# The dense products of a three-layer model kernel on one core: moving rows read, and accumulators written, from the last column to the first

## Chip, core and metric

One core of a Trainium2 chip runs the whole program in one launch. The metric is the device time of that launch in microseconds (us), the median of several executions. A profile is one further execution, recorded by the hardware profiler. In the profile PE is TensorE's matmuls, PEld its weight loads, DVE VectorE, ACT ScalarE, POOL GpSimd and SP the engine that issues most of the DMAs. Line numbers (L167) are lines of the kernel file.

## The reference

The input x is 1 x 1024 tokens x 1024 channels. Two blocks of a first model and one block of a second model follow one another, all in float32:

```python
for i in range(2):                       # first model
    xn  = rms_norm(h, norm_mix[i])
    mix = hawk_block(xn, ...) if i == 0 else rwkv7_time_mix(xn, ...)
    h = h + mix
    h = h + swiglu(rms_norm(h, norm_ffn[i]), ffn_w_in[i], ffn_w_out[i])
    h = h + (p[i] @ ple_w_proj[i]) * sigmoid(rms_norm(h, norm_ple[i]) @ ple_w_gate[i])
h = rms_norm(h, norm_final)
# second model, one block
proj = rms_norm(h, g) @ w_in             # split in u, z, q, k, v, z_attn
h = h + rms_norm(concat(s5(u) * silu(z), window_attention(q, k, v) * silu(z_attn)) @ w_out, g2)
h = h + sigmoid(h @ w_gate + b) * (p_2 @ w_proj)
```

Nearly all arithmetic lies in the `@` products with weights of 1024 to 2816 rows and up to 5632 columns, over 1024 tokens.

## The kernel before

**Layout.** Activations are held transposed: channels on the 128 partitions, the T = 1024 tokens along the free dimension, one row tile of 128 channels after another (`[P, KD, T]`). A dense product takes 128 x 128 pieces of the weight as the stationary operand and a row tile of activations as the moving operand, in two halves of HALF = 512 tokens, each of which goes to one accumulator bank of 128 x 512 float32 in `g.ps`.

**Three passes.** To keep near-float32 accuracy with the one-pass float32r format, each weight is split into a high and a low part (`whi`, `wlo`) and each activation as well (`xh`, `xl`). A product is the sum of whi x xh, whi x xl and wlo x xh. So for each 128 x 128 piece of weight there are six matmuls: three passes times two halves, all into the same pair of banks.

**Four places issue them.** `product` (L167) serves the projections of all blocks; `unit` (L416) the last blocks of a product whose sum of squares is taken on the way, and the output product of the feed-forward network; `combined` (L1047) the input product of the feed-forward network, written as a Strassen-like scheme of seven products on sums and differences of quarters, each in one half (`x[n][:, k, :]` has 512 columns); `piece` (L2423) the first pieces of the RWKV output product, between the steps of the recurrence. All other matmuls (`ident`, `head_mean`, the recurrence, the attention, the state space model) are written out elsewhere with float32 or bfloat16 operands.

**What sets the order.** Each engine has its own instruction list, written by hand, with semaphore waits. SP loads weight blocks in pairs (`load_blocks`, L106), POOL splits them (`split_blocks`, L117 to L120) once the block before the last is done, ACT and DVE make the high and low rows of the activations and read the finished accumulators. Two pairs of banks take turns (`banks(g, 2 * s)`, s = 0 or 1), so one is read while the other fills.

**Two other products matter for what follows.** In the state space model, `steps(ap)` views a row of 1024 tokens as four interleaved sequences, every fourth token:

```python
def steps(ap):
    return ap.rearrange("p (c j) -> p j c", j=STEP)      # STEP = 4, 256 tokens each
```

`s5_drive_pe` (L3561) streams such a row of 256 tokens as the moving operand, with 32 partitions as contraction, four in different row groups of the array. `within` (L3599) streams one or two of them (256 or 512 columns) over all 128 partitions. Both are float32, both step 4 elements, 16 bytes, from one token to the next, and both write contiguous columns. `across` (L3612) reads 255 contiguous float32 columns and writes 255 contiguous columns of a bank from an odd column on (`i % 2 * NCH + 1`).

Of the kernel before, what the change touches and what calls it, by code (L numbers as in the profile page):

```python
# [13 lines left out]
P = 128  # L14
T = 1024
D = 1024
KD = D // P
HALF = 512
# [137 lines left out]
        nc.tensor.matmul(g.ps[:, b, :], g.ident[:, 0:P // 2].bitcast(BF16), rows, start=True, stop=True)  # L156


def product(nc, g, s, units, xh, xl, acc, at=0, ready=None, start=True, stop=True):

    for kt in range(units):
        if ready is not None:
            ready(kt)
        c = (at + kt) * P
        for n, (w, x) in enumerate(((g.whi, xh), (g.whi, xl), (g.wlo, xh))):
            for hf in (0, 1):
                last = nc.tensor.matmul(acc[:, hf, :], w[:, s, c:c + P], x[:, kt, hf * HALF:(hf + 1) * HALF],  # L167
                                        start=start and kt == 0 and n == 0, stop=stop and kt == units - 1 and n == 2)
    return last


def paired(pe, nc, g, first, units, xh, xl, acc, tail=None, between=None, lead=0):

    pe.wait_ge(g.w_split.sem, first + 2)
    pe.wait_ge(g.acc_free.sem, first)
    keep_busy(nc, g, 7, lead)
    for kt in range(units):
        pe.wait_ge(g.x_split.sem, g.x_split.base + kt + 1)
        for s in (0, 1):
            last = product(nc, g, s, 1, xh[:, kt:kt + 1, :], xl[:, kt:kt + 1, :], acc[s], at=kt, start=kt == 0, stop=kt == units - 1)  # L180
            if kt == units - 1:
                if s == 1 and tail is not None:
                    last = tail()
                last.then_inc(g.block_done.sem, 1)
        if between is not None and kt == KD // 2:
            between()
# [16 lines left out]
def banks(g, b):  # L203

    return g.ps[:, b:b + 2, :]
# [49 lines left out]
def sums_pe(pe, nc, g):  # L255

    pe.wait_ge(g.sq_used.sem, g.sq_used.base + KD)
    for j in range(NT):
        ins = nc.tensor.matmul(g.ps[:, 6, j:j + 1], g.sumsq[:, j * P:(j + 1) * P], g.ones[:, 0:1], start=True, stop=True)  # L259
        if j == NT // 2 - 1:  # L260
            keep_busy(nc, g, 7, 2)
    ins.then_inc(g.ss_done.sem, 1)


def spread_pe(pe, nc, g, tmp):

    pe.wait_ge(g.diag_ready.sem, g.diag_ready.base + 1)
    for hf in (0, 1):
        ins = nc.tensor.matmul(g.ps[:, 6 + hf, :], g.ones[:], flat(tmp.diag[:, 4 * hf:4 * hf + 4, :]), start=True, stop=True)  # L269
    ins.then_inc(g.bc_done.sem, 1)  # L270
# [140 lines left out]
def unit(nc, g, s, at, hi, lo, acc, start, stop):  # L411

    c = at * P
    for n, (w, x) in enumerate(((g.whi, hi), (g.whi, lo), (g.wlo, hi))):
        for hf in (0, 1):
            last = nc.tensor.matmul(acc[:, hf, :], w[:, s, c:c + P], x[:, hf, :], start=start and n == 0, stop=stop and n == 2)  # L416
    return last


# [116 lines left out]
def hawk_in(nc, g, block, m):  # L536
# [33 lines left out]
    def _(pe):  # L570
# [18 lines left out]
        for kt in range(1, KD):  # L589
            if kt == KD // 2:  # L590
                spread_pe(pe, nc, g, tmp)
            ins = unit(nc, g, 1, kt, halves(xh[:, kt, :]), halves(xl[:, kt, :]), banks(g, 2), False, kt == KD - 1)
# [309 lines left out]
def tile_slot(i):  # L902
    return i % FFN_SLOTS


def ffn(nc, g, block, mem, layer):
# [25 lines left out]
    def slot(n):  # L932
        if n in whole:
            h, l, at = whole[n]
            return h[:, at, :], l[:, at, :]
        s, c = shared[n]
        return g.whi[:, s, c:c + HALF], g.wlo[:, s, c:c + HALF]
# [6 lines left out]
    acc = {n: g.ps[:, 4 + n % 4, :] for n in range(PAIR)}  # L944
# [93 lines left out]
    @block.tensor  # L1038
    def _(pe):
        def combined(m, n, acc, ready=None):  # L1040
            hi, lo = slot(n)
            pe.wait_ge(g.weight_low.sem, m * PAIR + (g.weight_low.base - PAIR + n + 1))
            for k in range(KD // 2):
                if ready is not None:
                    pe.wait_ge(g.t_low.sem, g.t_low.base + ready + k + 1)
                for i, (w, x) in enumerate(((hi, mem.hi), (hi, mem.lo), (lo, mem.hi))):
                    last = nc.tensor.matmul(acc, w[:, k * P:(k + 1) * P], x[n][:, k, :], start=k == 0 and i == 0, stop=k == KD // 2 - 1 and i == 2)  # L1047
            last.then_inc(g.product_done.sem, 1)

        def pair(m, ready):  # L1050
            pe.wait_ge(g.fourth_part.sem, m + (g.fourth_part.base - 1))
            combined(m, A11, acc[A11])
            pe.wait_ge(g.up_part.sem, m * 2 + g.up_part.base)
            combined(m, S2_, acc[S2_], ready.get(T2_))
            pe.wait_ge(g.gate_sum.sem, m * 2 + g.gate_sum.base)
            combined(m, A12, acc[A12])
            pe.wait_ge(g.third_part.sem, m + (g.third_part.base - 1))
            combined(m, S3_, acc[S3_], ready.get(T3_))
            pe.wait_ge(g.first_part.sem, m + g.first_part.base)
            combined(m, S1_, acc[S1_], ready.get(T1_))  # L1060
            pe.wait_ge(g.second_part.sem, m + g.second_part.base)
            combined(m, A22, acc[A22], ready.get(T4_))
            pe.wait_ge(g.gate_sum.sem, m * 2 + (g.gate_sum.base + 1))
            combined(m, S4_, acc[S4_])

        def out_block(grp, s, kt_ready=None, kt_used=None, acc=None):
            tiles = tiles_of[grp]
            for n, i in enumerate(tiles):
                if kt_ready:
                    pe.wait_ge(g.tile_low.sem, g.tile_low.base + i + 1)  # L1070
                at = tile_slot(i)
                last = unit(nc, g, s, n, mem.tile_hi[at], mem.tile_lo[at], acc, n == 0, n == len(tiles) - 1)
                if kt_used and n < len(tiles) - 1:
                    last.then_inc(g.tile_used.sem, 1)
            last.then_inc(g.block_done.sem, 1)

        pe.wait_ge(g.w_split.sem, first + 1)
        pe.wait_ge(g.acc_free.sem, first - 1)
        for kt in range(KD):
            if kt == KD - 2:  # L1080
                sums_pe(pe, nc, g)
            pe.wait_ge(g.x_split.sem, g.x_split.base + kt + 1)
            last = unit(nc, g, 0, kt, rows.hi[kt], rows.lo[kt], banks(g, 0), kt == 0, kt == KD - 1)
        last.then_inc(g.block_done.sem, 1)
        pe.wait_ge(g.w_split.sem, first + 2)
        pe.wait_ge(g.acc_free.sem, first)
        for kt in range(KD):
            if kt == 2:
                spread_pe(pe, nc, g, tmp)
            last = unit(nc, g, 1, kt, rows.hi[kt], rows.lo[kt], banks(g, 2), kt == 0, kt == KD - 1)  # L1090
        last.then_inc(g.block_done.sem, 1)
        pe.wait_ge(g.rstd_ready.sem, g.rstd_ready.base + 1)
        pair(1, {T2_: 0, T3_: 4, T1_: 8, T4_: 12})
        with pe.Fori(2, last_pair + 1) as m:
            pair(m, {})
        for grp, fo in enumerate(first_out):
            def wait_block(q, s):
                pe.wait_ge(g.w_split.sem, q * 2 + (fo + s + 1))
                pe.wait_ge(g.acc_free.sem, q * 2 + (fo + s - 1))

            wait_block(0, 0)
            out_block(grp, 0, kt_ready=True, acc=banks(g, 0))
            wait_block(0, 1)
            out_block(grp, 1, acc=banks(g, 2))
            with pe.Fori(1, KD // 2 - 1) as q:
                for s in (0, 1):
                    wait_block(q, s)
                    out_block(grp, s, acc=banks(g, 2 * s))
            wait_block(KD // 2 - 1, 0)
            out_block(grp, 0, acc=banks(g, 0))  # L1110
            wait_block(KD // 2 - 1, 1)
            out_block(grp, 1, kt_used=grp == 0, acc=banks(g, 2))
# [936 lines left out]
def rw_core(nc, g, block, nxt, small, mk, xh, xl):  # L2049
# [19 lines left out]
    sw, a, r, kx, v, c, e1, e2, kk, t1 = (nxt[:, n, :] for n in range(10))  # L2069
    at, bt, kt, rt = (now[:, n, :] for n in range(4))  # L2070
# [140 lines left out]
    def _(pe):  # L2211
# [206 lines left out]
        def piece(s, i):  # L2418
            kt, n, hf = i // 6, i % 6 // 2, i % 2
            if i % 6 == 0:  # L2420
                pe.wait_ge(g.x_split.sem, g.x_split.base + kt + 1)
            w, x = ((g.whi, xh), (g.whi, xl), (g.wlo, xh))[n]
            nc.tensor.matmul(banks(g, 2 * s)[:, hf, :], w[:, s, kt * P:(kt + 1) * P], x[:, kt, hf * HALF:(hf + 1) * HALF],  # L2423
                             start=kt == 0 and n == 0, stop=False)

        pe.wait_ge(g.y1_ready.sem, g.y1_ready.base + KD)
# [8 lines left out]
        for i in range(30, 36):  # L2435
            piece(0, i)
# [1914 lines left out]
```

## Time and profile before

| | |
|---|---|
| median of 3 executions | 3548.92 us (3545.87 to 3551.94) |
| the profiled execution's own time | 3547.82 us |
| its span, first to last instruction | 3546.0 us |
| mean granted TensorE clock over the span | 0.982 of full speed |
| PE busy | 3405.1 us, 96% of the span |
| PEld / DVE / POOL / ACT busy | 78% / 56% / 45% / 34% |

The span and the time differ by 1.8 us, which lies around the program. PE is the busiest engine by far in every stage. A matmul's row in the trace has a start and a duration; matmuls overlap in the pipeline, so the duration of one says how long it takes through the array, and the distance between starts of neighbours says what one costs in a stream.

### The profile page before, as it was taken

Reading aid. Unit: us, or ns where it says so; the run is one execution under the profiler, and the core shown is the slowest. Engines: PE = TensorE matmul, PEld = TensorE weight load, DVE = VectorE, ACT = ScalarE, POOL = GpSimd, SP = SyncE. Lnnn points to the kernel's source line nnn. Section 1 sums busy time; section 2 is a strip of 40 time slices with the busy share of each in tenths; the row PEclk is TensorE's granted clock in tenths of the full one; section 3 lists DMA queues with packets and bytes.
Section 4 is the critical chain, followed back from the end, with each engine's and each line's share of the span. In section 5 each row is a group of like instructions: output and inputs, shape, how many; then the busy total and the mean of one; then the engine's idle time right before and its main releaser. Section 6 shows DMA issues by size and latency. Waiting matters only on the chain. (4 is left out here: it accounts for less than half of the span.)

```text
span 3546.0 us, 61071 instructions
## 1 busy us (share of the span) xinstructions
PE 3405.1 (96%) x25028; PEld 2748.4 (78%) x25028; DVE 1984.6 (56%) x2398; ACT 1194.9 (34%) x1597; POOL 1590.5 (45%) x1148
## 2 busy tenths in 40 slices
PE   7998999999999999999999999999999999999989
PEld 5886778888888777888787877888888887674767
DVE  6886565556224652226767647555542458868452
ACT  4654233333102362226465524333310231242221
POOL 3442377775333323334344425877633323560352
PEclk9998999999999999999999999999999999999999
DMA  2111122224311142241212211222332113111212
GB/s 103 48 49 38 33 87 79 80 89 152 109 42 56 40 179 95 95 147 39 85 46 86 68 37 48 88 89 78 111 128 88 52 42 119 61 48 42 101 43 76
DMA packets 74063, 274.58 MB, mean 77 GB/s; under 512 B 8208, under 2 KB 8592, under 8 KB 73360
## 3 DMA queue, kind: packets, MB, share of 16 engines
q1 hardware_dynamic: 68112, 250.79, 20.8%
q10 hardware_dynamic: 5760, 20.97, 1.5%
q8 instruction: 153, 2.51, 0.3%
q14 instruction: 38, 0.31, 0.0%
HBM read 207.77 MB, written 63.96 MB: 77 GB/s over the span
## 5 line engine op out<-in xcount | busy, mean ns | idle before, releaser
L117 POOL TENSOR_TENSOR gap<-ones 128x1 f32<-128x1 f32 x150 | 46.0, 307 | 1238.8 <-PE ps L167 774.4
L120 POOL TENSOR_TENSOR wlo<-wraw,whi 128x1024 fp32r<-128x1024 f32 (+3 forms) x150 | 391.6, 2611 | 12.5
L893 DVE TENSOR_TENSOR h<-ps,h 128x1024 f32<-128x1024 f32 (+1 forms) x56 | 68.5, 1223 | 288.9 <-PE ps L416 259.6
L167 PE MATMUL ps<-xh,whi 128*128 128x512 f32 x640 | 203.0, 399 | 21.6 <-ACT rw_stage L1888 5.1
L167 PE MATMUL ps<-xl,whi 128*128 128x512 f32 x640 | 199.2, 393 | 0.0
L167 PE MATMUL ps<-xh,wlo 128*128 128x512 f32 x640 | 198.7, 392 | 0.0
L1007 POOL TENSOR_TENSOR wlo<-wraw,whi 128x512 fp32r<-128x512 f32 x126 | 166.3, 1335 | 52.6 <-ACT whi L1130 52.6
L118 POOL TENSOR_SCALAR whi<-wraw 128x1024 fp32r<-128x1024 f32 (+3 forms) x150 | 178.9, 1192 | 0.0
L384 ACT ACTIVATE sq<-h 128x1024 f32<-128x1024 f32 x32 | 34.0, 1061 | 394.1 <-DVE h L893 304.0
L2200 POOL TENSOR_TENSOR rw_levels<-rw_levels,rw_masks 128x512 f32<-128x512 f32 x64 | 87.2, 1378 | 177.2 <-PE ps L2289 140.8
L167 PEld LDWEIGHTS ps<-xh,whi 128*128 128x128 f32 x640 | 119.7, 190 | 56.6 <-issue 8.9
L1007 POOL TENSOR_TENSOR ffn_wl<-ffn_wsum,ffn_wh 128x512 fp32r<-128x512 f32 x84 | 111.6, 1328 | 110.7 <-ACT ffn_wh L1130 110.6
L167 PEld LDWEIGHTS ps<-xl,whi 128*128 128x128 f32 x640 | 121.3, 190 | 25.9
L167 PEld LDWEIGHTS ps<-xh,wlo 128*128 128x128 f32 x640 | 121.2, 189 | 25.8
L1288 DVE TENSOR_TENSOR sum_of_squares<-ffn_part,sq 128x512 f32<-128x512 f32 x84 | 132.6, 1578 | 9.3
L1130 ACT ACTIVATE whi<-wraw 128x512 fp32r<-128x512 f32 x126 | 79.2, 630 | 168.9 <-POOL wraw L1002 90.3
L1047 PE MATMUL ps<-xh_sums,whi 128*128 128x512 f32 x336 | 130.9, 390 | 2.2 <-ACT ffn_part L1143 2.2
L1047 PE MATMUL ps<-xh_sums,wlo 128*128 128x512 f32 x336 | 130.7, 389 | 0.0
L1047 PE MATMUL ps<-xl_sums,whi 128*128 128x512 f32 x336 | 130.7, 389 | 0.0
L433 DVE TENSOR_TENSOR sum_of_squares<-sum_of_squares,sq 128x1024 f32<-128x1024 f32 x48 | 93.7, 1951 | 56.9 <-ACT sq L384 38.7
L416 PE MATMUL ps<-xh_sums,whi 128*128 128x512 f32 x384 | 118.4, 390 | 0.4 <-POOL wlo L120 0.4
L416 PE MATMUL ps<-xh_sums,wlo 128*128 128x512 f32 x384 | 118.3, 389 | 0.0
(673 smaller groups left out, 9535.0 us busy)
## 6 DMA issues: line engine op xcount, KB each, us to landing
wraw<-w_ffn_in SPq DMA_DIRECT2D x88, 512.0 KB, 3.5
ffn_hidden<-sum_of_squares SPq DMA_DIRECT2D x44, 512.0 KB, 2.6
rw_next<-rw_kept SPq DMA_DIRECT2D x40, 512.0 KB, 5.1
wraw<-w_ffn_out SPq DMA_DIRECT2D x32, 512.0 KB, 3.6
ffn_stage<-ffn_hidden SPq DMA_DIRECT2D x30, 512.0 KB, 4.9
rw_kept<-rw_stage SPq DMA_DIRECT2D x24, 512.0 KB, 2.7
rw_kept<-rw_stage ACTq DMA_DIRECT2D x24, 512.0 KB, 2.7
wraw<-w_ple SPq DMA_DIRECT2D x16, 640.0 KB, 3.8
```

Of the source, the lines that this page charges most:

```text
L117: nc.gpsimd.tensor_tensor(g.gap[:, 0:1], g.ones[:, 0:1], g.ones[:, 0:1], ALU.mult)
L118: nc.gpsimd.tensor_scalar(g.whi[:, s, 0:w], g.wraw[:, s, 0:w], 1.0, 0.0, ALU.mult, ALU.add).then_inc(g.w_hi.sem, 1)
L120: nc.gpsimd.tensor_tensor(g.wlo[:, s, 0:w], g.wraw[:, s, 0:w], g.whi[:, s, 0:w].bitcast(F32), ALU.subtract).then_inc(g.w_split.sem, 1)
L167: last = nc.tensor.matmul(acc[:, hf, :], w[:, s, c:c + P], x[:, kt, hf * HALF:(hf + 1) * HALF], start=start and kt == 0 and n == 0, stop=s ...
L416: last = nc.tensor.matmul(acc[:, hf, :], w[:, s, c:c + P], x[:, hf, :], start=start and n == 0, stop=stop and n == 2)
L433: nc.vector.tensor_tensor(g.sumsq[:], g.sumsq[:], sq[:, s, :], ALU.add).then_inc(g.sq_used.sem, 1)
L893: nc.vector.tensor_tensor(ht, flat(banks(g, acc + 2 * s)), ht, ALU.add).then_inc(g.acc_free.sem, 1)
L1007: nc.gpsimd.tensor_tensor(packed(lo), raw[n], packed(hi).bitcast(F32), ALU.subtract).then_inc(g.weight_low.sem, 1)
L1047: last = nc.tensor.matmul(acc, w[:, k * P:(k + 1) * P], x[n][:, k, :], start=k == 0 and i == 0, stop=k == KD // 2 - 1 and i == 2)
L1130: nc.scalar.activation(packed(slot(n)[0]), raw[n], ACT.Copy).then_inc(g.weight_high.sem, 1)
L1288: nc.vector.tensor_tensor(hid[:, hf * HALF:(hf + 1) * HALF], (u3, up1)[hf], gated[hf], ALU.mult).then_inc(g.half_ready.sem, 1)
L2200: nc.gpsimd.tensor_tensor(halved(Nm[:, h]), twice(Nc[:, h]), mask_wide(f"off{b}"), ALU.mult).then_inc(g.off_ready.sem, 1)
```

## The change

A helper `turned` reverses the free dimension of an access pattern. The four places that issue the dense products apply it to the moving operand and to the accumulator. Column 511 of the moving half is read first and its result goes to column 511 of the bank, and so on down to column 0. The stationary operand, the number of instructions, their order, all waits and all readers of the accumulators stay as they are: compared without line numbers, the instruction lists of all engines are the same before and after.

```diff
+def turned(ap):
+
+    return ap[:, ::-1]
+
+
 def product(nc, g, s, units, xh, xl, acc, at=0, ready=None, start=True, stop=True):
...
-                last = nc.tensor.matmul(acc[:, hf, :], w[:, s, c:c + P], x[:, kt, hf * HALF:(hf + 1) * HALF],
+                last = nc.tensor.matmul(turned(acc[:, hf, :]), w[:, s, c:c + P], turned(x[:, kt, hf * HALF:(hf + 1) * HALF]),
...
-            last = nc.tensor.matmul(acc[:, hf, :], w[:, s, c:c + P], x[:, hf, :], start=start and n == 0, stop=stop and n == 2)
+            last = nc.tensor.matmul(turned(acc[:, hf, :]), w[:, s, c:c + P], turned(x[:, hf, :]), start=start and n == 0, stop=stop and n == 2)
...
-                    last = nc.tensor.matmul(acc, w[:, k * P:(k + 1) * P], x[n][:, k, :], start=k == 0 and i == 0, stop=k == KD // 2 - 1 and i == 2)
+                    last = nc.tensor.matmul(turned(acc), w[:, k * P:(k + 1) * P], turned(x[n][:, k, :]), start=k == 0 and i == 0, stop=k == KD // 2 - 1 and i == 2)
...
-            nc.tensor.matmul(banks(g, 2 * s)[:, hf, :], w[:, s, kt * P:(kt + 1) * P], x[:, kt, hf * HALF:(hf + 1) * HALF],
+            nc.tensor.matmul(turned(banks(g, 2 * s)[:, hf, :]), w[:, s, kt * P:(kt + 1) * P], turned(x[:, kt, hf * HALF:(hf + 1) * HALF]),
                              start=kt == 0 and n == 0, stop=False)
```

## Rows read from the trace of the kernel before

**Rows 1.** The page, busy time of each engine: us, share of the span, instructions.
```profile
span 3546.0 us, 61071 instructions
PE 3405.1 (96%) x25028; PEld 2748.4 (78%) x25028; DVE 1984.6 (56%) x2398; ACT 1194.9 (34%) x1597; POOL 1590.5 (45%) x1148
```

**Rows 2.** Windows: length, busy us (instructions) by engine, granted clock, DMA share, GB/s.
```profile
700.00:1300.00 600.00, 586.36 (x2579) 478.18 (x2578) 291.38 (x276) 172.45 (x203) 258.12 (x197) 1.00 0.26 90
1600.00:2060.00 460.00, 426.24 (x11426) 365.45 (x11419) 316.61 (x588) 249.08 (x365) 177.53 (x114) 0.94 0.19 63
2060.00:2900.00 840.00, 830.68 (x3664) 684.00 (x3663) 429.62 (x449) 229.82 (x322) 449.58 (x346) 1.00 0.24 80
```

**Rows 3.** Waits of PE: waiter <- releaser, us in total, times, longest.
```profile
PE ps L167 <- POOL wlo L120: 17.1, 5, 6.6
PE ps L156 <- PEq L3962: 11.9, 1, 11.9
```

**Rows 4.** Windows over the whole span, by line: L167, L1047, L416, then L2423.
```profile
0.00:3546.00 3546.00, 1256.77 (x5328) 1008.41 (x5328) 0.98 0.23 77
...
0.00:3546.00 3546.00, 802.43 (x3528) 661.64 (x3528) 0.98 0.23 77
...
0.00:3546.00 3546.00, 726.76 (x3168) 594.71 (x3168) 0.98 0.23 77
...
0.00:3546.00 3546.00, 21.14 (x72) 12.35 (x72) 0.98 0.23 77
```

**Rows 5.** Timeline of PE in the feed-forward product: start us, duration us, what.
```profile
600.16 0.39 PE L1047 MATMUL ps<-xl_even,ffn_wh 128*128 128x512 f32 x1
600.39 0.39 PE L1047 MATMUL ps<-xh_even,ffn_wl 128*128 128x512 f32 x1
...
611.72 0.39 PE L1047 MATMUL ps<-xl_sums,whi 128*128 128x512 f32 x1
611.95 0.39 PE L1047 MATMUL ps<-xh_sums,wlo 128*128 128x512 f32 x1
```

**Rows 6.** The chain that ended last, in order of time: start, us, what.
```profile
3421.03 21.41 POOL h L3884 x7
...
3456.94 81.91 PE ps L167 x360
...
3541.50 1.23 DVE h L3950
```

**Rows 7.** Timeline of PE, float32 products on contiguous rows.
```profile
2955.94 1.88 PE L3078 MATMUL ps<-sum_of_squares,ones 128*128 128x512 f32 x4
2957.66 1.88 PE L3078 MATMUL ps<-b_high,ones 128*128 128x512 f32 x4
```

**Rows 8.** Timeline of PE, state space model.
```profile
3217.69 9.25 PE L3599 MATMUL ps<-b_low,s_kernel 128*128 128x512 f32 x12
3226.87 3.65 PE L3612 MATMUL ps<-s_state,s_ct 128*32 128x255 f32 x64
...
3197.68 3.82 PE L3561 MATMUL ps<-b_low,h 32*128 32x256 f32 x32
```

**Rows 9.** By line: durations ns min/median/max, first and last start, forms.
```profile
L3599 PE MATMUL ps<-b_low,s_kernel x48: 629/1078/1147, 3217.7 to 3279.5; 128*128 128x512 f32 x32, 128*128 128x256 f32 x16
L3078 PE MATMUL ps<-sum_of_squares,ones x4: 591/592/592, 2955.9 to 2957.2; 128*128 128x512 f32 x4
L3561 PE MATMUL ps<-b_low,h x256: 624/627/692, 3197.2 to 3257.5; 32*128 32x256 f32 x128
L3150 PE MATMUL ps<-h,at_vtok x120: 379/379/430, 3053.9 to 3183.0; 128*64 128x256 f32 x120
L3612 PE MATMUL ps<-s_state,s_ct x256: 378/378/635, 3226.9 to 3286.7; 128*32 128x255 f32 x128
```

## The prediction, made before the changed kernel ran

> **What bounds the kernel now.** I read the busy time of each engine first. PE is busy for 3405.1 of 3546.0 us [rows 1]. The windows say that this is no average over unlike stages: PE is busy for 586.36 of 600 us in the Hawk output and feed-forward part, 830.68 of 840 us in the second layer's feed-forward and what follows, and even in the recurrence of the RWKV block, with 11426 small matmuls, 426.24 of 460 us [rows 2]. The clock is granted in full in the first and the last of these and at 0.94 in the recurrence. All that PE does not use is 3546.0 - 3405.1 = 141 us, in many short pieces: the largest total is 17.1 us for the low weights that POOL makes, the next 11.9 us before the first matmul [rows 3]. So the question is what the dense matmuls cost in a stream, and how many there are.
>
> How many: 5328 + 3528 + 3168 + 72 = 12096 [rows 4]. What one costs: in the feed-forward product the starts run from 600.16 to 611.95 us over 52 matmuls, 11.79 / 52 = 0.2267 us each [rows 5]. The 0.39 us beside each start is the time through the array, and is no cost in a stream. At the end of the program the chain of waits holds 360 of them in one piece of 81.91 us, 0.2275 us each, with only short DVE and ACT work behind [rows 6]. Together 12096 x 0.2267 = 2742 us: 81% of PE's busy time and 77% of the span are dense products, which sit on the path that sets the end nearly everywhere. Whatever one of them gains or loses is multiplied by 12096, and hardly anything hides it: 0.59 ns each is 7.1 us, 0.2% of the time, which is about what a measurement of this kernel can tell from no change.
>
> How near they are to the plain streaming rate: four float32 records of 128 x 512, each of which streams its 512 columns in two passes, start at 2955.94 and the next four at 2957.66 us, so one takes 0.430 us, a pass of 512 contiguous columns 0.215 us [rows 7]. That float32 record really is two passes is read from durations: 592 ns at 512 columns against 379 ns at 256, a difference of 213 ns for 512 column passes [rows 9]. A dense matmul at 0.2267 us is one such pass and 12 ns more. It has no slack in its stream: if the operand is delivered more slowly, the matmul is slower by just that.
>
> **The change, part by part.** No instruction is added, removed or moved, and no wait changes. DMAs, the work of DVE, ACT and POOL, and the stationary loads are as before. Three things change inside each of the 12096 matmuls.
>
> (a) The moving half is read downwards. The trace has no row of a downward read, so I bound it by its neighbours. The upper end is the moving operand that steps by 16 bytes. The state space products at L3599 have 12 records from 3217.69 us on, 8 of 512 and 4 of 256 columns, a width of ten records of 512; the next product starts at 3226.87 us [rows 8, 9]. That is 9.18 / 10 = 0.918 us for one of 512 columns; taken only to the start of the last record (3217.69 + 9.25 - 0.63 = 3226.31, 9.5 widths) it is 0.907. I take 0.91, against 0.430 on contiguous rows. The durations say the same: 1078 against 592 ns [rows 9]. Per pass of 512 columns that is 0.455 against 0.215, or +0.24 us. The product at L3561, also at step 16 bytes, has 32 records in 3.82 us, so (3.82 - 0.63) / 31 = 0.103 us each; four run beside each other in row groups, so four records of 2 x 256 column passes take 0.412 us [rows 8], +0.20 us on 0.215. The lower end is nothing: a backward row uses all four words of every 16 bytes, like a forward row and unlike the stepped one. If what costs is that each element lies in 16 bytes of its own, direction costs nothing; if what gives the full rate is an operand recognised by its step of exactly one word, a step of minus one is like any other and costs +0.20 to +0.24 us.
>
> (b) The accumulator is written downwards, on 12096 instructions, two thirds or more of which add to what is there. Here the trace has one row that speaks. L3612 writes from an odd column on, so that its neighbouring columns fall across pairs of words, and adds to the bank. Its 64 records take 3.65 us, (3.65 - 0.38) / 63 = 0.0519 us each, four beside each other in column groups: 0.208 us for 510 column passes, the full rate [rows 8], and its duration of 378 ns is the 379 ns of the aligned product at L3150 [rows 9]. So the writer doesn't need an even start for its rate. A backward write has the same two words in each pair, in the other order. Between no cost and a write that takes each word alone (half the rate, +0.21 us by the 0.215 us of a pass) I take no cost.
>
> (c) The start of each operand moves to the other end of its row. That could cost or save a fixed time per instruction. The nearest row is the 12 ns by which a dense matmul exceeds a bare pass [rows 5, 7]; I bound it by -12 and +12 ns and take 0, since the odd start of L3612 shows no fixed cost either.
>
> The sum that I forecast: 12096 x (0 + 0 + 0) = 0. The profiled execution's own time, 3547.82 us, stays, and it stands 1.1 us below the median of the three runs, so I predict the median, 3549 us.
>
> **A rule that speaks against it.** The row for writes in which neighbouring words don't follow upwards in a pair is L3612, at the full rate. The Trainium skill, page "PSUM — Partial Sum Buffer", Specifications, says of PSUM's 8-byte lines that "any non-contiguous AP slows matmuls significantly". Read by the letter, a pattern with step -1 is not a contiguous one, and the change would pay on each matmul; that reading is rival 1. The same skill, page "SBUF — State Buffer", in the passage on SBUF cachelines, gives the reason as accesses that stay in one line of 16 bytes, at least two per line, which a backward row does; by it the sum stays at 0. The stepped rows at about half the rate agree with both, and no row separates them.
>
> **Rival 1: the backward stream runs at the stepped rate (slower).** Place: inside every dense matmul, on the read, the write or both. For it: step 16 bytes does cost +0.20 to +0.24 us per 512 columns, and no row shows a negative step at the full rate. Against it: what the stepped rows lack, several elements per 16 bytes, the backward rows have, and the writer takes an odd start for free. Price: 12096 x 0.24 = 2903 us, so 3548 + 2903 = 6451 us; by L3561's 0.20 us it is 2419 us and 5967 us. The other engines would have slack and some of PE's 141 us of waits would close, at most that. It decides as soon as 30 of the 12096 matmuls run at this rate (30 x 0.24 = 7.2 us, 0.2%); since all have the same form, it is all or none: near 0, or 2.4 to 2.9 ms.
>
> **Rival 2: a small fixed price per instruction (slower).** The first fetch or the last write of a backward row could cost a cycle or more. The decision point is 0.59 ns each. A doubling of the 12 ns surplus would be 12096 x 0.012 = 145 us, 3693 us. More likely in this case is a nanosecond or two: 12 to 24 us, 3561 to 3573 us. Against it: the odd start of L3612 shows none.
>
> **Rival 3: the surplus goes (faster).** The 12 ns above a bare pass appear where a weight load runs under each matmul. If the moving stream and the weight load meet less often when one runs backwards, up to 145 us would go: 3404 us. Nothing in the trace points to it: the spacing is the same over all operands, in whatever place of memory they lie.
>
> **Rival 4: it doesn't do what it says.** If the reversal were dropped on both sides when the instruction is encoded, the result is the same and so is the time. It can't be told from the forecast by the time, and is counted with it.
>
> **How the numbers follow.** Forecast and rival 4: 0.73, at 3549 us, within 0.2%. Rival 1: 0.17, at 5970 to 6450 us. Rival 2: 0.07, at 3556 to 3693 us. Rival 3: 0.03, 3404 to 3541 us. So faster 0.03, same 0.73, slower 0.24. The range must leave out no more than 2 in 10: it takes the forecast with the spread of the runs before and rival 2 whole, 3538 to 3695 us, and leaves out rival 1 and most of rival 3. Likeliest alone: 3542 to 3556 us.
>
> **What would show each step.** In the profile after, dense rows of 0.39 us starting 0.227 us apart, PE busy 3405 us and the last 360 products in about 82 us say that (a) to (c) are right. Under rival 1 the durations would read 0.59 to 0.63 us, the starts 0.43 to 0.47 us apart, the loads of DVE, ACT and POOL would be unchanged and their shares nearly halved. Under rival 2 or 3 the spacing would differ from 0.2267 us in the third digit, alike on all four lines. The untouched rows, L3078 at 0.430 and L3599 at 0.91 us, should stay in every case. The prediction is wrong if the reader or the writer knows only an upward step as contiguous.

## The result: 1.8% slower, 6.7 ns on each dense matmul

| | before | after |
|---|---|---|
| median | 3550.43 us (3545.87 to 3556.33, 4 runs) | 3615.28 us (3613.18 to 3619.95, 4 runs) |
| ratio | | 1.0183, 95% interval 1.0165 to 1.0202 |
| span of the profiled execution | 3546.0 us | 3618.1 us |

The change costs 64.9 us between the medians, 72.1 us between the two profiled spans (the profiled execution of the changed kernel was the longest of its four). The page of the changed kernel, to be set beside [rows 1]:

```profile
span 3618.1 us, 61071 instructions
PE 3490.9 (96%) x25028; PEld 2759.5 (76%) x25028; DVE 1984.8 (55%) x2398; ACT 1194.8 (33%) x1597; POOL 1572.7 (43%) x1148
```

The instruction counts are the same on every engine, DVE and ACT are as busy as before, and PE has 85.8 us more. Its idle time shrank from 140.9 to 3618.1 - 3490.9 = 127.2 us, so 13.7 us of idle time closed while the products became slower. 85.8 - 13.7 = 72.1 us, the whole difference.

Where PE's time comes from is told by the windows over the span, by line, to be set beside [rows 4] (the lines are L172, L1052, L421 and L2428 now):

```profile
0.00:3618.10 3618.10, 1289.79 (x5328) 1011.88 (x5328) 0.98 0.22 76
...
0.00:3618.10 3618.10, 825.42 (x3528) 662.72 (x3528) 0.98 0.22 76
...
0.00:3618.10 3618.10, 748.11 (x3168) 596.55 (x3168) 0.98 0.22 76
...
0.00:3618.10 3618.10, 21.39 (x72) 12.38 (x72) 0.98 0.22 76
```

They rose by 33.0, 23.0, 21.4 and 0.2 us, 77.6 us together, that is 6.2, 6.5, 6.7 and 3.5 ns for each matmul. The mean granted clock was 0.982 before and 0.980 in this execution, 0.981 and 0.982 in the other three, so it is not the cause; it may be part of the 8.2 us that all other matmuls were busy longer (85.8 - 77.6). The timeline of the feed-forward product, the place of [rows 5] (first and last of 54 rows; start, duration, what):

```profile
599.62 0.40 PE L1052 MATMUL ps<-xh_sums,wlo 128*128 128x512 f32 x1
...
611.99 0.40 PE L1052 MATMUL ps<-xl_even,ffn_wh 128*128 128x512 f32 x1
```

12.37 us over 53 distances are 0.2334 us each, against 0.2267 before: +6.7 ns. The last 360 products in the chain of waits take 6.6 ns longer each, where [rows 6] have 81.91 us:

```profile
3526.67 84.29 PE ps L172 x360
```

12096 x 6.67 ns = 80.6 us is what the streams of dense products cost more; the rest of the way to 72.1 and 64.9 us is idle time that closed and the spread of the executions. The untouched product of [rows 8] still takes 9.25 us for its 12 records.

### The profile page after: what moved, and what is told of

Its sections match the earlier page's. It is cut to its first block and busy times, and to the rows that moved or that the text cites. A ratio compares the mean times of both kernels' runs of the same rounds, so it can differ in the third digit from the quotient of the medians.

```text
span 3618.1 us, 61071 instructions
## 1 busy us (share of the span) xinstructions
PE 3490.9 (96%) x25028; PEld 2759.5 (76%) x25028; DVE 1984.8 (55%) x2398; ACT 1194.8 (33%) x1597; POOL 1572.7 (43%) x1148
## 5 line engine op out<-in xcount | busy, mean ns | idle before, releaser
L172 PE MATMUL ps<-xh,whi 128*128 128x512 f32 x640 | 207.4, 406 | 20.1 <-ACT rw_stage L1893 4.9
L172 PE MATMUL ps<-xl,whi 128*128 128x512 f32 x640 | 204.2, 402 | 0.0
L172 PE MATMUL ps<-xh,wlo 128*128 128x512 f32 x640 | 204.1, 401 | 0.0
L172 PEld LDWEIGHTS ps<-xh,whi 128*128 128x128 f32 x640 | 120.5, 191 | 57.1 <-issue 8.1
L172 PEld LDWEIGHTS ps<-xl,whi 128*128 128x128 f32 x640 | 122.0, 191 | 29.8
L172 PEld LDWEIGHTS ps<-xh,wlo 128*128 128x128 f32 x640 | 121.9, 190 | 29.5
L1052 PE MATMUL ps<-xh_sums,whi 128*128 128x512 f32 x336 | 133.6, 398 | 0.4 <-ACT ffn_part L1148 0.4
L1052 PE MATMUL ps<-xl_sums,whi 128*128 128x512 f32 x336 | 133.5, 397 | 0.0
L1052 PE MATMUL ps<-xh_sums,wlo 128*128 128x512 f32 x336 | 133.5, 397 | 0.0
L438 DVE TENSOR_TENSOR sum_of_squares<-sum_of_squares,sq 128x1024 f32<-128x1024 f32 x48 | 92.7, 1932 | 56.8 <-ACT sq L389 38.6
L421 PE MATMUL ps<-xl_sums,whi 128*128 128x512 f32 x384 | 121.1, 397 | 0.0
L421 PE MATMUL ps<-xh_sums,wlo 128*128 128x512 f32 x384 | 121.1, 397 | 0.0
```

Source lines behind the costliest of these rows:

```text
L172: last = nc.tensor.matmul(turned(acc[:, hf, :]), w[:, s, c:c + P], turned(x[:, kt, hf * HALF:(hf + 1) * HALF]), start=start and kt == 0 an ...
L421: last = nc.tensor.matmul(turned(acc[:, hf, :]), w[:, s, c:c + P], turned(x[:, hf, :]), start=start and n == 0, stop=stop and n == 2)
L438: nc.vector.tensor_tensor(g.sumsq[:], g.sumsq[:], sq[:, s, :], ALU.add).then_inc(g.sq_used.sem, 1)
L1052: last = nc.tensor.matmul(turned(acc), w[:, k * P:(k + 1) * P], turned(x[n][:, k, :]), start=k == 0 and i == 0, stop=k == KD // 2 - 1 and ...
```

## Experiments

### Read or write?

Two kernels with one half of the change each. Both leave the columns of every dense product mirrored within their half, so their outputs are not the reference's, but they do the full work.

```diff
-    last = nc.tensor.matmul(turned(acc[:, hf, :]), w[:, s, c:c + P], turned(x[:, hf, :]), ...)
+    last = nc.tensor.matmul(acc[:, hf, :], w[:, s, c:c + P], turned(x[:, hf, :]), ...)          # read only
+    last = nc.tensor.matmul(turned(acc[:, hf, :]), w[:, s, c:c + P], x[:, hf, :], ...)          # write only
```

> Only the moving operand is read from the last column to the first; the accumulators are written forward, so within each half of 512 tokens every dense product lands mirrored and the output is not the reference's. The changed kernel's dense matmuls start 0.2334 us apart instead of 0.2267 (+6.7 ns). Theory R (the price is in the backward read): dense starts 0.233 us apart and +60 to +72 us over before, as in the changed kernel. Theory W (it is in the backward write): 0.2267 us apart, within 0.2% of before. Theory S (a share in each): about half, +30 to +36 us.

> Only the accumulators are written from the last column to the first, the moving rows are read forward; the products land mirrored within each half, so the output is not the reference's. Theory R: 0.2267 us apart, within 0.2% of before. Theory W: 0.233 us apart, +60 to +72 us. Theory S: +30 to +36 us. If the price is only paid where read and write directions agree, both this and the read-only kernel stay at before.

Read only: 3610.3 us against 3549.09, ratio 1.0173 (1.0156 to 1.0190). Write only: 3551.69 us, ratio 1.0004 (0.9994 to 1.0013). The price is in the backward read: 61.2 us of the 64.9, and the two ratios' intervals overlap. Writing the accumulator backwards costs nothing that these runs can see, with the operand read forward or backward, so theory R stands and W and S fall.

### Is it a price of each matmul, with nothing to hide it?

```diff
-  last = nc.tensor.matmul(acc, w[:, k * P:(k + 1) * P], x[n][:, k, :], ...)
+  last = nc.tensor.matmul(acc[:, ::-1], w[:, k * P:(k + 1) * P], x[n][:, k, :][:, ::-1], ...)
```

> Read and write backward in the feed-forward input product alone (3528 of the 12096 dense matmuls), the result is the reference's. If the price is one of each matmul and nothing hides it: 3528 x 6.7 ns = 24 us, less what idle time of PE takes up, so +18 to +24 us. If instead it is paid mostly elsewhere (at waits, in other stages): under +10 us.

3571.37 us, ratio 1.0063 (1.0046 to 1.0080), +22.3 us for 3528 of the matmuls. The full change has +64.9 us for 12096, which in proportion would be 18.9 us. So the price goes with the number of matmuls, and little hides it.

### What about the form of the access?

```diff
 def turned(ap):
-    return ap[:, ::-1]
+    return ap.rearrange("p (a b) -> p a b", a=2)[:, ::-1, :]
```

> In the place of backward columns all dense products read and write columns 256 to 511 first and then 0 to 255, both forward (the result is the reference's). If any change of the form of the access or of its first column costs, as much as the backward form or more: +60 us. If it is the negative step of the read: no difference, within 0.2% of before.

3549.84 us, ratio 0.9993 (0.9983 to 1.0002). Two runs of columns in swapped order cost nothing, so the change of the form is not the cause. Of another first column this run says less: column 256 lies 4 x 64 words on, and further below a shift by 64 words turns out to change nothing, while shifts by 1 to 48 words do.

### Streams of one kind of matmul

> The kernel before, unchanged in its result, with streams of 48 (float32: 24) matmuls of one kind each appended at its end, each on a line of its own. Base: forward read and write of 512 columns in float32r, expected 0.2267 us apart; both backward 0.2334. Theory F (a fixed price per instruction, for the start or end of a backward stream): at 256 columns the backward stream is also 6.7 ns dearer. Theory C (a slightly lower rate per column): at 256 columns half of it, 3.3 ns. Theory E (what costs is where a read starts in its line of memory): forward reads that start at the second, third or fourth word show the same price, and the backward ones that start there differ among themselves. Theory L (weight loads meet the backward stream): with one weight tile for all, the difference shrinks. A forward read at step 2 in 256 columns: 0.12 us apart if lines decide, 0.23 if only step one is fast; at step 4 about 0.23 by the rows of L3599. bfloat16 and float32 streams: the same +6.7 ns if the price is the instruction's, nothing if it belongs to float32r.

Each stream is one row of the timeline, and the distance of two rows, divided by 48, is the cost of one matmul. Forward, backward, backward read alone, backward write alone, all 512 columns in float32r (the first holds a slow start, so the forward value of 226.7 ns is taken from the second forward stream of this kernel, with the accumulation started and stopped at each matmul):

```profile
3560.98 11.27 PE L164 MATMUL ps<-xh,whi 128*128 128x512 f32 x48
3572.09 11.37 PE L167 MATMUL ps<-xh,whi 128*128 128x512 f32 x48
3583.30 11.37 PE L170 MATMUL ps<-xh,whi 128*128 128x512 f32 x48
3594.50 11.06 PE L173 MATMUL ps<-xh,whi 128*128 128x512 f32 x48
3605.39 5.92 PE L176 MATMUL ps<-xh,whi 128*128 128x256 f32 x48
3611.15 5.85 PE L179 MATMUL ps<-xh,whi 128*128 128x256 f32 x48
3616.83 5.84 PE L182 MATMUL ps<-xh,whi 128*128 128x256 f32 x48
...
3639.32 11.04 PE L191 MATMUL ps<-xh,whi 128*128 128x512 f32 x48
3650.20 11.37 PE L194 MATMUL ps<-xh,whi 128*128 128x512 f32 x48
```

Backward 11.21 / 48 = 233.5 ns, backward read 233.3, backward write 226.9. L176 and L179 are 256 columns, forward 120.0 and backward 5.68 / 48 = 118.3 ns: here backward is the cheaper one. So it is not a fixed price of an instruction (theory F). Matmuls with forward and backward in turn cost 230.4 ns, half of the price. One weight tile for all, still loaded for each matmul, made no difference (227.1 and 233.3 ns), against what theory L expected. At 256 columns forward reads that start one, two and three words on cost 123.1, 126.5 and 116.7 ns: where a read starts counts, as theory E has it, and the reading in place is not the cheapest at this width. Backward reads that start there cost 120.0 ns each time. A float32r read at step 2, 256 columns, took 226.5 ns, twice the contiguous one.

The float32 streams show no price for a step of two in the write or for going backwards. Records of 256 columns, in two passes each: written contiguously, written at step 2, read and written backwards:

```profile
3762.52 10.54 PE L233 MATMUL ps<-h,ones 128*128 128x256 f32 x48
3772.90 10.52 PE L236 MATMUL ps<-h,ones 128*128 128x256 f32 x48
3783.26 10.52 PE L239 MATMUL ps<-h,ones 128*128 128x256 f32 x48
```

The first takes (3772.90 - 3762.52) / 48 = 216.3 ns a record, the second 215.8, and so does the third.

The second kernel of this kind swept the widths and the formats.

> The kernel before with other streams of 48 matmuls appended at its end (its result unchanged). At 256 columns the backward stream cost 118.3 ns a matmul against 120.0 forward, at 512 it costs 233.3 against 226.7, so the price is not one fixed amount. Theory C (a lower rate per column and a cheaper start): between 128 and 512 columns the backward stream lies on one line, about 0.449 ns per column and 3 ns, the forward one on 0.417 ns per column and 13.3 ns; they cross near 310 columns. Theory Q (the matmul's cost is rounded up to a grid, in which direction and start only move the point): forward and backward both jump in steps of 1.7 or 3.3 ns, and the difference changes sign more than once over the widths. Start offsets: at 256 columns forward reads that start one, two or three words into their 16 bytes cost 123.1, 126.5 and 116.7 ns. If this holds at 512, they cost 230.0, 233.3 and 223.3 ns, and four and eight words on it repeats the aligned 226.7; the backward ones move by no more than that. bfloat16: 215.9 forward and 220.4 backward at 512; under theory C the difference shrinks or turns at 128 and 256 columns. A write at step 2 or 4 of a one-pass product at 256 or 128 columns: 2 x or more the contiguous spacing if a step in the accumulator costs, the same if not.

448 and 512 columns forward, then the same backward; 256 columns forward from four (L257) and eight words on (L260); bfloat16 at 256 and 512 columns forward, at 256 and 512 backward:

```profile
3605.16 10.07 PE L182 MATMUL ps<-xh,whi 128*128 128x448 f32 x48
3615.07 11.09 PE L185 MATMUL ps<-xh,whi 128*128 128x512 f32 x48
3626.00 5.47 PE L188 MATMUL ps<-xh,whi 128*128 128x128 f32 x48
...
3657.97 10.08 PE L203 MATMUL ps<-xh,whi 128*128 128x448 f32 x48
3667.89 11.37 PE L206 MATMUL ps<-xh,whi 128*128 128x512 f32 x48
...
3859.00 5.76 PE L257 MATMUL ps<-xh,whi 128*128 128x256 f32 x48
3864.60 5.76 PE L260 MATMUL ps<-xh,whi 128*128 128x256 f32 x48
3870.21 2.85 PE L263 MATMUL ps<-xh,ident 128*128 128x128 bf16 x48
3872.90 5.40 PE L266 MATMUL ps<-xh,ident 128*128 128x256 bf16 x48
3878.14 10.52 PE L269 MATMUL ps<-xh,ident 128*128 128x512 bf16 x48
...
3891.18 5.40 PE L275 MATMUL ps<-xh,ident 128*128 128x256 bf16 x48
3896.42 10.52 PE L278 MATMUL ps<-xh,ident 128*128 128x512 bf16 x48
...
3912.22 10.52 PE L284 MATMUL ps<-xh,ident 128*128 128x256 bf16 x48
3922.53 5.45 PE L287 MATMUL ps<-xh,ident 128*128 128x128 bf16 x48
```

At 448 columns forward (206.5 ns) and backward (206.7) are equal, at 384 backward is dearer (177.7 against 173.5), at 320, 192 and 128 they are equal. A line per column (theory C) does not pass through these. Theory Q, a cost that jumps and a direction that moves the jump, fits them better, but the difference changes its sign once and not several times, so it isn't shown either. In bfloat16 the duration of a stream of 48 is 10.52 us of 512 columns in either direction, and at 128 and 256 columns the two directions agree within 0.2 ns: no price at these widths. The L284 row is a bfloat16 product of 256 columns written at step 2: (3922.53 - 3912.22) / 48 = 214.8 ns against 109.2 contiguous. So in bfloat16 the accumulator's writer has a price for a step of two and none for a step of minus one. At 512 columns, float32r, none of eight forward offsets of the read (1 to 8 words) reached the unshifted value: 230.0 to 239.8 ns, so the expectation that four and eight words on would repeat it failed. At 256 columns it is the other way round: four and eight words on cost 116.7 and 116.9 ns, less than the 120.2 in place. Backward with offsets: 233.3 to 239.8 ns.

### The read against the weights

> The kernel before with other streams of 48 float32r matmuls of 512 columns appended at its end (its result unchanged), forward and backward reads apart. [...] Theory L (the backward row meets the fetch of the next matmul's weights): with 64 or 32 stationary columns instead of 128, the load is shorter, and the difference of 6.7 ns and most of the 11 ns by which a forward float32r matmul exceeds a bfloat16 one (226.7 against 215.8) go; shifting the weights by 1 to 64 words changes both directions by some ns. Theory A (the reader alone, whatever the weights do): backward stays at 233.3 and forward at 226.7 with any number and place of stationary columns. Order in groups of G columns: if the price comes from the order of words inside 8 or 16 bytes, groups forward with columns backward inside them (G = 2, 4) cost as much as backward, and backward groups with columns forward inside cost nothing; if it comes from the order in which lines are visited, the other way round.

Rows in order: weights in place, forward and backward; then weights 16 words on, forward and backward:

```profile
3573.58 11.04 PE L167 MATMUL ps<-xh,whi 128*128 128x512 f32 x48
3584.46 11.37 PE L170 MATMUL ps<-xh,whi 128*128 128x512 f32 x48
...
3729.37 11.37 PE L209 MATMUL ps<-xh,whi 128*128 128x512 f32 x48
3740.57 11.36 PE L212 MATMUL ps<-xh,whi 128*128 128x512 f32 x48
```

With the weights 16 words on, a plain forward read costs (3740.57 - 3729.37) / 48 = 233.3 ns, what the backward one costs, and the backward one stays. At 1, 2 and 4 words forward is 232.5, 230.6 and 233.5 ns, at 64 words 227.1 again; backward is 233.3 to 233.5 at each of the five shifts. Theory A, the reader alone, is out. The part of theory L about the length of the load failed: with 64 or 32 stationary columns forward rose to 230.4 and 231.7 ns and backward stayed at 233.1.

The order in groups of columns, read backward group by group with the columns inside forward, cost 233.3 ns for groups of 2, 4, 8 and 16 and 227.3 for groups of 64. Groups forward with the columns backward inside cost 226.7 for 2 and 4, but 232.9 for 8, 266.7 for 16 and 233.7 for 64:

```profile
3818.67 11.07 PE L233 MATMUL ps<-xh,whi 128*128 128x512 f32 x48
3829.58 11.04 PE L236 MATMUL ps<-xh,whi 128*128 128x512 f32 x48
3840.46 11.04 PE L239 MATMUL ps<-xh,whi 128*128 128x512 f32 x48
3851.34 11.35 PE L242 MATMUL ps<-xh,whi 128*128 128x512 f32 x48
3862.52 12.96 PE L245 MATMUL ps<-xh,whi 128*128 128x512 f32 x48
3875.32 11.38 PE L248 MATMUL ps<-xh,whi 128*128 128x512 f32 x48
3886.54 11.06 PE L251 MATMUL ps<-xh,whi 128*128 128x512 f32 x48
```

(groups of 64 backward; then 2, 4, 8, 16, 64 inside backward; the last row only ends the one before it.) The order of the words within 16 bytes is free, and so is the order of stretches of 64 columns (256 bytes). What costs is the order in which the 16-byte pieces inside such a stretch are visited. Why groups of 16 cost so much more than the rest stays open.

> The kernel before with 54 streams of 48 float32r matmuls of 512 columns at its end (its result unchanged): forward reads that start 0 to 64 words on, against weights fetched 0 to 64 words on, and six backward ones. The read alone (theory A) gives one value per read offset, the same for every weight offset. Theory L (what counts is how the moving read and the weight fetch lie against each other in memory) gives a table in which rows and columns both matter: 226.7 ns at (0, 0) and (64 words, 0), 233.3 at (16 words, 0) as measured, and the moving offset can make up for the weight offset; values repeat with a period of 64 words. Backward: 233.3 wherever the two lie, if its meeting is the general case and the forward 226.7 ns the favourable one. If some pair lies below 226.7 ns, the kernel before has something to gain there: 12 us per ns.

Forward reads, ns a matmul, worked out from the distances of the rows; across, by how many words the read starts later, down, by how many the weights do:

| | 0 | 4 | 8 | 16 | 24 | 32 | 48 | 64 |
|---|---|---|---|---|---|---|---|---|
| 0 | **226.7** | 231.5 | 233.5 | 228.8 | 233.8 | 233.1 | 233.3 | **227.3** |
| 8 | 233.1 | 226.9 | **227.5** | 233.3 | 229.2 | 233.5 | 234.2 | 233.1 |
| 16 | 233.3 | 234.6 | 233.3 | **226.7** | 233.5 | 229.0 | 232.5 | 233.1 |
| 32 | 232.5 | 233.1 | 234.0 | 233.1 | 233.1 | **226.7** | 229.4 | 232.3 |
| 48 | 233.5 | 231.0 | 233.3 | 232.5 | 234.2 | 233.3 | **227.1** | 229.4 |
| 64 | **226.9** | 231.7 | 233.5 | 228.8 | 233.5 | 233.3 | 233.3 | **227.1** |

Some of its rows: weights 8 on with the read 4 and then 8 on, weights 16 on with the read in place, both 16 on:

```profile
3671.52 11.05 PE L194 MATMUL ps<-xh,whi 128*128 128x512 f32 x48
3682.41 11.08 PE L197 MATMUL ps<-xh,whi 128*128 128x512 f32 x48
...
3749.17 11.36 PE L215 MATMUL ps<-xh,whi 128*128 128x512 f32 x48
...
3782.83 11.05 PE L224 MATMUL ps<-xh,whi 128*128 128x512 f32 x48
```

The low values lie on the diagonal and come back after 64 words (256 bytes). In the unshifted kernel the program places every dense product's moving row and weights at addresses with the same remainder modulo 256 bytes (in the last block `whi` at byte 47712 of a partition and `xh` at 105056, both 96 above a multiple of 256), so the diagonal is where the two start at the same place modulo 64 words. There the forward read costs 226.7 to 227.5 ns, and 231 to 234.6 nearly everywhere else. There are exceptions: one pair off the diagonal (weights 8, read 4) is as cheap, 226.9 ns, and a read 16 words ahead of the weights costs 228.8 to 229.4. So the same place is enough for the low price, but it is not the only one that has it. Six backward streams gave 233.3 to 236.7 ns. No pair lies below 226.7, so there was nothing to gain over the kernel before.

### The same price without a backward access

```diff
-  g.whi = ctx.enter_context(nc.sbuf_tensor("whi", [P, 2, WMAX], F32R))
+  g.whi = ctx.enter_context(nc.sbuf_tensor("whi", [P, 2 * WMAX + 64], F32R))[:, 16:16 + 2 * WMAX].rearrange("p (s w) -> p s w", s=2)
```

and the same for `wlo`; the control has `0:2 * WMAX`.

> The kernel before, all reads and writes forward, the result the reference's; only the two tiles of split weights (whi, wlo) lie 16 words (64 bytes) further on in memory, in tiles padded by 64 words so that everything behind them keeps its place modulo 64 words. Theory L (the 6.7 ns are lost whenever the forward read and the weight fetch don't start at the same place modulo 64 words, and the backward read is merely the general case): the 10584 dense matmuls whose weights lie in these tiles start 0.233 us apart, the 1512 with weights in ffn_wh and ffn_wl stay at 0.2267, and the time rises by about 10584/12096 of the change's +65 us: +50 to +62 us, without any backward access. Theory A (only the direction of the read counts): within 0.2% of before.

> The same padded tiles with the weights at their start, so that nothing moves modulo 64 words (result the reference's). Both theories: 0.2267 us apart, within 0.2% of before. If the padding itself, or the absolute place, costs: as much as the shifted kernel.

Shifted: 3606.14 us against 3550.32, ratio 1.0161 (1.0143 to 1.0178), +55.8 us, all reads forward. Padded only: ratio 1.0004 (0.9994 to 1.0014). The rise of 55.8 us is 10584 / 12096 of the 64.9 us (56.8) within the noise. In the shifted kernel's timeline, weights in `whi` and `wlo` first, then in `ffn_wh` and `ffn_wl`, which had not moved:

```profile
599.61 0.39 PE L1047 MATMUL ps<-xl_sums,whi 128*128 128x512 f32 x1
...
604.75 0.39 PE L1047 MATMUL ps<-xh_even,wlo 128*128 128x512 f32 x1
604.98 0.39 PE L1047 MATMUL ps<-xh_odd,ffn_wh 128*128 128x512 f32 x1
...
611.81 0.39 PE L1047 MATMUL ps<-xh_sums,ffn_wh 128*128 128x512 f32 x1
```

5.14 us over 22 distances are 233.6 ns, 6.83 over 30 are 227.7 ns. One line of code has both prices, by the place of its weights.

> The changed kernel (read and write backward) with the split weights 16 words further on as well; the result is the reference's. Shifting the weights alone gave +55.8 us, the backward access alone +64.9 us. Theory L (both lose the same favourable meeting of read and weight fetch, which can be lost only once): dense matmuls 0.233 us apart, +60 to +70 us over before. If the two are separate prices that add up: 0.239 us apart where the weights lie in the shifted tiles, about +120 us.

3612.39 us against 3549.61, ratio 1.0174 (1.0153 to 1.0195), +62.8 us. The two don't add up: the shift takes nothing more from a kernel that reads backwards. Nor does the load itself take longer: in the feed-forward product the weight loads' own rows have a median of 188 ns in the kernel before, in the changed and in the shifted one.

## Why the prediction was right and wrong

**The range held, the forecast didn't.** 3615.28 us lies between 3538 and 3695. But the likeliest case, no change, with 0.73, is out. What came has the size of rival 2, which had 0.07 and to which the upper end of the range belonged; its likelier case, 12 to 24 us, was too small. And it has that rival's size alone, not its mechanism: a cost of the first fetch or the last write of each instruction would be there at 256 columns too, where backward was cheaper by 1.7 ns. That the range holds the result is luck of a wide bound.

**What bounds the kernel: right.** PE carries the time and little hides a change of its stream. The dense lines' busy time rose by 77.6 us and the span by 72.1; 13.7 us of PE's idle time closed, and the other matmuls' busy time differed by 85.8 - 77.6 = 8.2 us between the two executions. The count of 12096 held, and the busy time changed nearly alike on the three large lines (6.2 to 6.7 ns a matmul), as foreseen for rival 2.

**(b), the write: right, but by luck.** Taken as free, it is (1.0004). The row that it rested on, the odd start of L3612, could not tell: it is a float32 product, and a float32 product is not slowed even by a write at step 2 (215.8 against 216.3 ns a record, L236 and L233 of the first stream kernel), which doubles a bfloat16 one. The page "PSUM — Partial Sum Buffer" of the Trainium skill says in its Specifications that any non-contiguous pattern slows matmuls significantly. That fits a step of two in bfloat16 (214.8 against 109.2 ns), not a step of two in float32, and not a step of minus one.

**(a), the read, at the same rate: right in that it didn't fall to the stepped rate.** Rival 1, with 0.17, did not come. Its counter-argument, that an element needs company within its 16 bytes, is not a sound one: at step 2 two words share 16 bytes, and a float32r read still took 226.5 ns for 256 columns. The page "SBUF — State Buffer" of the Trainium skill, in its passage on cachelines, lets fp32 stride by 4 elements for free; this row speaks against it for float32r, while a bfloat16 read at step 2 cost 113.3 against 109.2 ns.

**(c), the fixed part: the step that failed.** I bounded it by 12 ns on either side and took 0, "since the odd start of L3612 shows no fixed cost either". That row is a float32 product that writes at an odd place; it says nothing of how a float32r read lies against its weights. In its place the runs show a term of 6.67 ns, a little over half of the bound, and it is not a fixed part of an instruction: it comes from how the moving read lies and runs against the weights. I priced only what the changed operand does by itself. The surplus of 12 ns over a bare pass, which I had seen in [rows 5, 7], could have been a reason to ask what else takes part in the stream; that the weights cause it is not shown, and a bfloat16 stream with its own loads beneath it has none (215.8 ns). Likewise rival 3's sentence that the spacing is the same "in whatever place of memory they lie": the tiles lie at different places, but all at the same place modulo 256 bytes, and so the spacing shows only what this one favourable case gives.

**What the runs show and what they don't.** Shown: the price is in the read; a backward read has it in float32r at 512 columns and not in bfloat16 or float32; a forward float32r read of 512 columns has or lacks it by its place against the weights, which repeats after 64 words; the same price can be had forward by moving the weights, and it is paid once. Argued, not shown: that it is a collision of the two fetches in the same part of memory, and that the backward read costs what it does for the same reason as a shifted forward one (equal price and no sum are the evidence). Open: why shorter weight loads didn't lower it, why the pair (8, 4) is cheap, and why at 256 columns other places are the favourable ones (116.7 ns four words on, 118.3 backward, 120.0 in place). In bfloat16 only the direction was varied, not the place of the weights.

## What to carry to other kernels

Where nearly all time is one instruction repeated 12096 times, a few ns that depend on placement are worth 1.6 to 1.8 per cent: measure the spacing of a short stream of exactly that instruction before a change of access pattern or of memory layout. In a float32r product of 512 columns keep the moving operand and the weights at the same place modulo 256 bytes, and read forward; at another width measure first, since at 256 columns this place cost 3 ns more than one four words on. The accumulator may be written in either direction; a step of two doubled a bfloat16 product. A row of another format is no evidence: the float32 rows showed no price for writes that bfloat16 pays for. Price a change of one operand by what shares the stream with it, not by the changed operand alone.

## What the runs showed of the hardware that was not expected

A float32r matmul of 512 columns took 226.7 ns with the read and the weights starting at the same place modulo 64 words, and mostly about 233.3 ns otherwise (one of the other pairs, 226.9); reading all columns backwards gave 233.1 ns or more in every such stream. Moving the split weights' tiles by 64 bytes made the kernel 1.6% slower. The Trainium skill, page "TensorE: Matmul & The Clock Gate", Part 2, says that loading the next tile's weights "doesn't steal SBUF read bandwidth from the running matmul"; for float32r the shifted kernel speaks against it, since the place of the weights alone cost 55.8 us, though no row shows that it is bandwidth that is lost. A bad order can cost more than a backward one: columns backward inside groups of 16 took 266.7 ns. A float32 product had no price for a write at step 2, a bfloat16 one took twice as long.
